# mLSTM stage of a hybrid decoder step: the rows of running maxima go to all partitions by two DMAs instead of by matmuls

## The reference, cut to what matters

```python
def step(carry, inp):
    C, n, m = carry
    qc, kc, vc, ic, fc = inp
    b = jnp.cumsum(fc, axis=-1)
    logw = jnp.where(causal, b[..., :, None] - b[..., None, :] + ic[..., None, :], -jnp.inf)
    inter = b + m[..., None]
    mt = jnp.maximum(inter, jnp.max(logw, axis=-1))
    s = jnp.einsum('bhtd,bhsd->bhts', qc, kc) * jnp.exp(logw - mt[..., None])
    wi = jnp.exp(inter - mt)
    num = wi[..., None] * jnp.einsum('bhtd,bhde->bhte', qc, C) + jnp.einsum('bhts,bhse->bhte', s, vc)
    ...
```

## Time and profile before

| what | us |
|---|---|
| median of 3 runs | 2701.71 |
| lowest and highest of them | 2697.43, 2702.18 |
| span of the profiled execution | 2697.6 |
| busy in it: TensorE | 2461.4 |
| VectorE | 1864.8 |
| ScalarE | 911.2 |
| GpSimd | 403.5 |

### The profile page before, as it was taken

One profiled execution on the slowest core, in us unless ns is written; L12 is line 12 of the kernel. 1 busy time (PEld: TensorE's weight loads), 2 busy tenths in 40 slices (PEclk: granted clock), 3 DMA queues, 4 the chain that ended last, 5 costly groups with the idle time before them and its releaser, 6 DMA issues. The chain is left out here.

```text
span 2697.6 us, 44581 instructions
## 1 busy us (share of the span) xinstructions
PE 2461.4 (91%) x17104; PEld 1521.1 (56%) x17104; DVE 1864.8 (69%) x3831; ACT 911.2 (34%) x1383; POOL 403.5 (15%) x384
## 2 busy tenths in 40 slices
PE   3899999879989999599969999999999998889997
PEld 1455555567667786455536666666666663334443
DVE  4555555446888886578867777777767668787666
ACT  1433333214444444144432222222222224332222
POOL 0132322300000000012242212221222200000000
PEclk7999999989999999699989999999999999999999
DMA  7434443460242311333412221222122217543323
GB/s 260 154 106 140 160 144 109 141 204 21 86 159 102 132 55 38 114 125 108 133 45 74 80 75 49 73 79 75 50 78 73 75 47 237 183 145 106 106 86 94
DMA packets 209320, 291.36 MB, mean 108 GB/s; under 512 B 19727, under 2 KB 146239, under 8 KB 207027
## 3 DMA queue, kind: packets, MB, share of 16 engines
q1 hardware_dynamic: 208933, 289.72, 33.0%
q10 hardware_dynamic: 270, 0.10, 0.0%
HBM read 214.48 MB, written 75.29 MB: 107 GB/s over the span
## 5 line engine op out<-in xcount | busy, mean ns | idle before, releaser
L2586 PE MATMUL py<-h_parts,w_heads 128*128 128x384 f16 (+1 forms) x792 | 246.0, 311 | 19.6 <-DVE u_p L2741 19.6
L2587 PE MATMUL py<-h_parts,w_heads 128*128 128x384 f16 (+1 forms) x792 | 245.8, 310 | 0.0
L2588 PE MATMUL py<-h_parts,w_heads 128*128 128x384 f16 (+1 forms) x792 | 245.8, 310 | 0.0
L336 PE MATMUL prj<-w_heads,h_parts_t 128*128 128x512 f16 x512 | 195.8, 382 | 12.6 <-PEq L451 6.2
L337 PE MATMUL prj<-w_heads,h_parts_t 128*128 128x512 f16 x512 | 195.6, 382 | 0.0
L338 PE MATMUL prj<-w_heads,h_parts_t 128*128 128x512 f16 x512 | 195.3, 382 | 0.0
L336 PE MATMUL m_prj<-m_h,w_heads 128*128 128x128 f16 (+1 forms) x1088 | 179.1, 218 | 12.5 <-DMA m_h<-h_parts 11.2
L2586 PE MATMUL px<-h_parts,w_heads 128*128 128x384 f16 (+1 forms) x528 | 164.4, 311 | 17.5 <-PEq L1884 17.5
L337 PE MATMUL m_prj<-m_h,w_heads 128*128 128x128 f16 (+1 forms) x1088 | 179.1, 217 | 0.0
L338 PE MATMUL m_prj<-m_h,w_heads 128*128 128x128 f16 (+1 forms) x1088 | 179.0, 217 | 0.0
L2587 PE MATMUL px<-h_parts,w_heads 128*128 128x384 f16 (+1 forms) x528 | 164.5, 311 | 0.0
(11 more groups left out here) (553 smaller groups left out, 6022.6 us busy)
## 6 DMA issues: line engine op xcount, KB each, us to landing
C_new<-in_w_up_dram SPq DMA_DIRECT2D x11, 2048.0 KB, 7.6
w_heads<-in_w_up_dram SPq DMA_DIRECT2D x44, 512.0 KB, 5.5
d_a<-act_cols SPq DMA_DIRECT2D x174, 128.0 KB, 2.4
act_cols<-w_heads SPq DMA_DIRECT2D x44, 384.0 KB, 2.4
win_raw<-in_w_ada_dram SPq DMA_DIRECT2D x8, 2048.0 KB
first_a<-in_w_down_dram SPq DMA_DIRECT2D x22, 512.0 KB, 3.8
first_a<-in_w_down_dram SPq DMA_DIRECT2D x44, 256.0 KB, 3.4
wa<-in_w_ada_dram SPq DMA_DIRECT2D x4, 2048.0 KB, 11.3
```

Source lines behind the costliest of these rows:

```text
L336: nc.tensor.matmul(out, left[0], right[0], start=(k == 0), stop=False)
L2586: nc.tensor.matmul(out, left[0], right[0], start=(start and k == 0), stop=False, skip_group_check=True)
L2587: nc.tensor.matmul(out, left[0], right[1], start=False, stop=False, skip_group_check=True)
L2588: last = nc.tensor.matmul(out, left[1], right[0], start=False, stop=(k == KC // 2 - 1), skip_group_check=True)
```

## The change

Each chunk's row MX is stored to a small tensor in device memory (4 rows of 128 floats, 2 KB), and read back into a new SBUF tile `mx` of 128 partitions, each of which gets all 512 floats (256 KB). Both DMAs are issued by SyncE in `spread_max(c)`, which waits for `ma`, issues the store, waits until the readers of the tile's last content are done and the store has landed, and issues the load. In SyncE's list `spread_max(c + 1)` stands ahead of `save_y(c)`. The matmuls of L1384 and the semaphore `arg_done` go; `mask_exponent` and `state_weight` read `mx` and wait for `mx_in`. `decay_exp` works in place in `dm`, and the tile that it filled before gives its room to `mx`. `rows_in`, which overwrites the gate tile, waits for the store of the last MX.

```diff
+        self.mx = nc.dram_tensor("max_row", [NCH + 1, H, P], F32, kind="Internal").ap()
...
-        dexp = sb("decay_exp", [P, H, P])
+        mx = sb("max_rows", [P, H, P])
...
+            def spread_max(c):
+
+                sp.wait_ge(s["ma"], c + 1)
+                sp.dma_start(core.mx[bass.ds(c, 1)].rearrange("o h t -> (o h) t"), r[:, MX, :]).then_inc(s["mx_saved"], 16)
+                sp.wait_ge(s["arg_here"], c)
+                sp.wait_ge(s["wi_here"], c)
+                sp.wait_ge(s["mx_saved"], 16 * c + 16)
+                sp.dma_start(mx[:], core.mx[bass.ds(c, 1)].broadcast_to([P, H, P])).then_inc(s["mx_in"], 16)
+
...
             load_piece(0)
+            spread_max(0)
             load_h(2, 0, P)
             load_h(3, 1, P)
 
             def step(i, pieces=True):
                 for u in range(2):
+                    spread_max(2 * i + u + 1)
                     save_y(2 * i + u, P)
                     load_h(2 * i + u + 4, u, P)
                     if pieces:
...
+            spread_max(NCH - 3)
             save_y(NCH - 4, P)
             load_h(NCH, 0, NS)
+            spread_max(NCH - 2)
             save_y(NCH - 3, P)
+            spread_max(NCH - 1)
             save_y(NCH - 2, P)
+            spread_max(NCH)
             sp.wait_ge(prep.parts_free, 16 * 3)
...
-                for i in range(H):
-                    last = pe.matmul(att[:, 1, i * P:i * P + T], heads[:, i, :], r[:, MX, 0:T], start=True, stop=True)
-                last.then_inc(s["arg_done"], 1)
...
             def rows_in(c, T):
 
                 act.wait_ge(s["gates_done"], c + 1)
-                act.wait_ge(s["arg_done"], c)
+                act.wait_ge(s["mx_saved"], 16 * c)
...
                 act.wait_ge(s["arg_here"], c + 1)
+                act.wait_ge(s["mx_in"], 16 * c + 16)
                 for i in range(H):
-                    last = nc.scalar.activation(wi[:, i, :], att[:, 1, i * P:(i + 1) * P], ACT.Exp, scale=-1.0, bias=tk[:, 3 * H + i:3 * H + i + 1])
+                    last = nc.scalar.activation(wi[:, i, :], mx[:, i, :], ACT.Exp, scale=-1.0, bias=tk[:, 3 * H + i:3 * H + i + 1])
...
             def decay_exp(c, T):
                 act.wait_ge(s["arg_here"], c + 1)
-                act.wait_ge(s["probs_here"], c)
-                nc.scalar.activation(dexp[0:T, :, 0:T], dm[0:T, :, 0:T], ACT.Exp, scale=-1.0).then_inc(s["dexp"], 1)
+                nc.scalar.activation(dm[0:T, :, 0:T], dm[0:T, :, 0:T], ACT.Exp, scale=-1.0).then_inc(s["dexp"], 1)
...
             def mask_exponent(c, T, mfar):
-                dve.wait_ge(s["arg_done"], c + 1)
+                dve.wait_ge(s["mx_in"], 16 * c + 16)
                 dve.wait_ge(s["tk_here"], c + 1)
                 for i in range(H):
-                    last = nc.vector.scalar_tensor_tensor(out=dm[0:T, i, 0:T], in0=att[0:T, 1, i * P:i * P + T], scalar=tk[0:T, 2 * H + i:2 * H + i + 1],
+                    last = nc.vector.scalar_tensor_tensor(out=dm[0:T, i, 0:T], in0=mx[0:T, i, 0:T], scalar=tk[0:T, 2 * H + i:2 * H + i + 1],
```

More of the change, by code:

```diff
@@ L1232, in phase_mls @@
             "const h_in0 h_in1 mq_done mk_done v_done g_done gates_done mb_here mbt_here tap0 conv tanh2 qk_here v_here "
-            "rows_in xf_abs soft ma rows_here tk_turned tk_here k_turned ktw_here arg_done arg_here dexp "
+            "rows_in xf_abs soft ma rows_here tk_turned tk_here k_turned ktw_here arg_here dexp "
             "wia_done wi_here qwi_here scores_done probs_here o_done s_done state_here var_here rstd_here y_here "
-            "y_saved g_tanh gate steps consts_here state_in mrows_turned mrows_here nrow_turned nrow_here "
+            "y_saved g_tanh gate steps consts_here state_in mx_saved mx_in mrows_turned mrows_here nrow_turned nrow_here "
             "qm_here km_here sb_done sb_here mt_here mt_turned mout_here saved dec_done pool_ask pool_all piece_in piece_maxed ".split())}
@@ L1709, in probs @@
                 dve.wait_ge(s["o_done"], c)
-                nc.vector.scalar_tensor_tensor(out=pr[0:T, :, 0:T], in0=of_heads(att[0:T, 0, :], T), scalar=QK_SCALE, in1=dexp[0:T, :, 0:T], op0=ALU.mult, op1=ALU.mult).then_inc(s["probs_here"], 1)
+                nc.vector.scalar_tensor_tensor(out=pr[0:T, :, 0:T], in0=of_heads(att[0:T, 0, :], T), scalar=QK_SCALE, in1=dm[0:T, :, 0:T], op0=ALU.mult, op1=ALU.mult).then_inc(s["probs_here"], 1)
             def norm_y(c, T, steps):
```

## The result

| | before | after |
|---|---|---|
| median of the runs | 2701.94 us (2697.43 to 2702.40, 4 runs) | 2829.17 us (2827.73 to 2837.61, 4 runs) |
| span of the profiled execution | 2697.6 us | 2827.2 us |
| mean granted TensorE clock | 0.960 | 0.936 |

The change makes the kernel slower: ratio 1.0484, 95% interval 1.0468 to 1.0500, or 127.2 us. The forecast was 2822.4 us.

What follows compares the result with a forecast made beforehand. Prediction: VectorE bounds chunks 2 to 11, TensorE chunks 0, 1, 13, 14 and 15. Stall 126.0 less 5.3 for matmuls gives +120.7 on 2697.6, 2818.3; with 4.1 for the median of runs, 2822.4 us, range 2790 to 2862.

Steps and rivals of the forecast that it cites:

- The mechanism: In chunks 2 to 11 SyncE's order holds the store behind find_max and the 2 MB piece, stalling mask_exponent; chance 0.76.
- Rival C: In SyncE's queue the 2 MB piece delays neither DMA: 43 us less 5.3, 2739 us; chance 0.04.
- rival A: The small store slips past the piece, only the load stands behind it: +98.2 us, 2799.9 us; chance 0.10.
- D: Not slower: the stall falls into time VectorE waits for TensorE anyway, 2684 us; 0.04 together with the stall never forming.
- The stall: VectorE at mask_exponent in ten chunks waits for store and load: 126.0 us in all, some 10.8 in an ordinary chunk.
- y's 7.8: Median landing time of the saving of y behind the piece, taken for the store in seven of ten chunks.
- lands 0.6 us sooner: Upper bound on how much earlier than y the 2 KB store behind the piece may land; 0.3 was taken.
- L1384: Eight matmul passes removed per chunk save 1.06 us each in chunks 0, 1, 12, 13 and 14: 5.3 us.
- ScalarE's operand: Reading SBUF instead of PSUM in state_weight's four exponentials costs ScalarE zero, at most 5 us in ten chunks.
- Hidden parts: DMAs in chunks 0, 1 and 12 to 16, later h loads and output weights cost zero; 5 us if not.
- TensorE's clock: TensorE's cold start after each stalled chunk's pause costs the path 0 us.
- Rival B: TensorE's clock stays low longer, reaching VectorE by gates or outputs: 3.3 us in ten chunks, +33, 2855 us; chance 0.06.

Runs made afterwards that it cites:

- e1: The changed kernel with both DMAs of a chunk moved ahead of the 2 MB weight piece in SyncE's list; 2703.93 us, ratio 1.0012 to before.
- e4: The changed kernel with 44 unused matmuls of 512 columns filling TensorE's pause in chunks 2 to 11; 2823.96 us, ratio 1.0466 to before.
- e5: The kernel before the change with the four matmuls of L1384 issued twice in every chunk; 2716.38 us, ratio 1.0058.
- e6: The changed kernel with ScalarE instead of SyncE issuing both DMAs; 2704.95 us, ratio 1.0009 to before.
- e10: The changed kernel with 56 unused four-column matmuls in TensorE's pause ahead of the stage's first load of h; 2829.53 us.
- e12: The very same kernel as e10, executed once more with its profile; 2823.43 us.

## Why the prediction was right, point by point

**The mechanism** held in every part: ten stalls, chunks 2 to 11 and no other, each on the DMA into max_rows; SyncE issuing the store 0.4 us after find_max; nothing in chunks 0, 1 and 12 to 16. e1 shows that the order alone makes the difference of 125 us. Rival C (the piece delays neither) is refuted by 7 us of flight, rival A (the store slips past the piece) by the same rows, and D by the 125.1 us of idle time.

**The stall**: 125.1 us measured, 126.0 forecast. That is closer than its terms deserve. From the old point of mask_exponent to the landing of the stores I had 95.5 us. Measured are 86.3 us of flight and some 4.7 us ahead of the issue (0.3 in an ordinary chunk, 1.3 and 0.8 in chunks 5 and 9, where the issues of two more transfers stand in between), so 91.0. An ordinary store took 6.9 to 7.3 us, against 7.5 taken from y's 7.8; chunk 3, for which y's 9.7 was taken, had 6.96; chunks 9 and 5 had 12.48 and 17.47 us against 13.2 and 18.2. The 2 KB are through before y's 256 KB would be: the bound "lands 0.6 us sooner" was nearer than the 0.3 that I took. The load went the other way: 3.14 to 3.57 us and 34.1 in all, against 30.5. Two misses of some 4 us cancel, which is luck.

The Trainium skill (DMA: Bandwidth & Descriptors, "Anatomy of one DMA") gives, as an estimate worked out from its fit, 2.6 us for this load. The trace does not agree: 3.3 us in the median where nothing is ahead of it (e1), and the row of y with 2.0 was no nearer.

**L1384**: forecast -5.3 us. Measured, the way to chunk 0 shrank by 0.97 us (from the first load of h to its mask_exponent, 44.09 to 43.12), and chunks 0, 1, 12 and 13 by 1.08, 0.24, 0.62 and 2.56: -5.5 in all. The sum is right, and the distribution is not: I had 1.06 five times. Chunk 13 seems to owe more to the clock than to eight passes. Its windows, before and after:

```profile
1016.00:1020.00 4.00, 4.00 (x12) 1.45 (x12) 2.41 (x6) 2.75 (x9) 0.38 (x1) 0.57 0.00 0
...
1142.00:1146.00 4.00, 4.00 (x20) 1.83 (x19) 2.42 (x6) 2.85 (x8) 0.38 (x1) 1.00 0.00 0
```

The clock was low there in the profiled execution of before and not in that of after; a dip of the same place and length costs e4 1.7 us. So an estimated 1.7 of the 5.5 us are luck, and the passes gave back about 3.8. The last stretch, from chunk 14 to the output phase, grew by 0.99 instead of shrinking.

**ScalarE's operand**, taken as zero with a bound of 5 us: the exponential from SBUF takes 386 ns in the median against a mean of 363, 4 x 0.023 = 0.09 us a chunk. In e1 chunks 3, 5 and 7 are 33.82, 33.74 and 33.82 us long against 33.73, 33.64 and 33.72, that is 0.1 each. So about 1 us. Going by VectorE's pair and not by L1508 was right.

**Hidden parts**, taken as zero: chunk 0's mask_exponent started at 615.26 against 615.33, with the load issued at 610.23 and landed 3.73 us later. The output weights left at 1212.01, as late as forecast, and the saves behind them; the output phase was not held up by more than the 0.99 us above. The zero was probably 0.8 too low: from the end of SyncE's last issue of the stage to the first instruction of the output phase it is 5.1 to 5.7 us in the three kernels that load the output weights early (before, e5, e6) and 6.0 to 7.0 in all others; in after 6.46 against 5.65. No run isolates it.

**TensorE's clock**: I took 0 from one pair of chunks, and this step was wrong, though by little. The clock was at 0.50 at the end of each of the ten stalls, and 2.9 us reached VectorE, by way of the gates. The earlier trace rows named only what VectorE itself waits for; it also waits for ScalarE's gate rows, and ScalarE for TensorE's gate projection. One warm and one cold chunk of equal length were too small a sample. Rival B had the right path (gates) and the wrong size, 3.3 us a chunk where 0.76 is the most that was seen. The rule of the Trainium skill (TensorE: Matmul & The Clock Gate, "HAM oscillation"), that a wait for data in a loop throttles in every round, agrees with the trace, in ten stalls of ten; its price of half the throttled time, estimated at 20 us, does not: ScalarE waited 2.9 us for the cold TensorE, and VectorE lost as much.

**Outside the stage** the forecast had nothing. There were 5.1 us in phases that no edit touches, and 0.9 ahead of the stage. By the sum, 120.7 forecast and 129.6 measured between the spans: the stall -0.9, L1384 -0.2, the cold starts +2.9, the end of the stage +1.0, the two later phases +5.1, the part ahead of the stage +0.9, together +8.8, or the 8.9 between the two before rounding. The 3.1 us of the up phase go with the clock: like e10, the changed kernel comes out of the start late (5.9 us into the phase, 2.9 before) and dips at L197. The 2.0 us of the down phase were not followed. In medians it is 127.2 against 120.7, since the profiled execution of before was one of the short ones; my 4.1 us for that were right for before and too much for after, whose median lies 2.0 us above its span.

## What to carry to other kernels

A DMA that is written behind another in one engine's list inherits that other's wait: ask of each place in the list what the issuing engine must have seen before it gets there, and place a small, early-ready transfer ahead of the large one that waits for the consumer. Here the same two DMAs cost 125 us behind the piece and 0 ahead of it. When a replaced operation was not on the path (eight matmul passes in chunks bound by VectorE), a free replacement gains nothing either; and differences of 3 to 5 us in this kernel want several executions, and a cut of the span by phases, before they are put down to an edit.

## What the runs showed of the hardware

A 2 KB store takes 1.23 us from issue to the next instruction that waited for it, and 6.9 to 7.3 when it is issued 0.38 us behind a 2 MB load, 12.5 and 17.5 behind two and three transfers of that size. A load of 256 KB broadcast to 128 partitions takes 3.3 us alone and about 5.0 when a 2 MB transfer is issued 0.38 us behind it.

The same pause of TensorE, 2.64 us, dropped its clock from 2.4 to 1.2 GHz in one execution of a kernel and not in another, and the time at the low level after a long pause differed too; one kernel's up phase took 850.5 or 853.7 us by this. The Trainium skill (TensorE: Matmul & The Clock Gate, "Part 1") says that the cold start of one kernel varies from run to run; e10 and e12 agree: TensorE comes out of the same wait of 17.5 us at the low clock, which ends 6.0 us into the up phase in one and 2.8 in the other. Their spans are 2831.2 and 2821.6 us. Of those 9.5 us, 3.2 are in the up phase, 4.5 in the stage, 0.5 in the down phase and 1.8 ahead of the stage; the output phase was 0.6 shorter. The clock was followed in the up phase and in chunk 16, not in the rest.
